# Expert slot numbers and gates fetched once ahead of the block loop; row gathers issued ahead of scatters; part of the last expert's first loads held back

## The reference, cut to what matters

```python
logits = (xf @ router_w + router_b)
top_vals, top_idx = lax.top_k(logits, TOP_K)          # 4 of 32 experts
gates = jax.nn.softmax(top_vals, axis=-1)
...
xb = xf[row_tok].reshape(n_blocks, MOE_BLOCK, D)      # rows of each expert, in blocks
h = xblk @ w1[e] + b1[e]                              # 1024 -> 2048
act = g * jax.nn.sigmoid(SWIGLU_ALPHA * g) * (u + 1.0)
y = act @ w2[e] + b2[e]                               # 1024 -> 1024
out = zeros.at[row_tok].add(y * row_w[:, None])
```

## Time and profile before

| | |
|---|---|
| median of 3 runs | 2829.48 us (2829.42 to 2830.85) |
| profiled execution | 2824.4 us |
| its span, first to last instruction | 2822.6 us |
| mean granted TensorE clock | 0.948 |
| PE busy | 2552.1 us (90%) |
| DVE, ACT, POOL busy | 744.7, 362.4, 499.3 us |
| bytes moved | 511.69 MB, mean 181 GB/s |
| routing ends, loop begins | about 985, 1009 us |
| last block's products end | about 2792 us |

### The profile page before, as it was taken

The page is one execution under the profiler, slowest core; times in us unless marked ns, Lnnn a source line. Parts: engine busy times, 40 slices in busy tenths (PEclk is TensorE's granted clock), DMA queues, the critical chain, the costliest instruction groups (busy, mean ns, idle before and its releaser), DMA issues.

```text
span 2822.6 us, 59253 instructions
## 1 busy us (share of the span) xinstructions
PE 2552.1 (90%) x22930; PEld 1090.6 (39%) x22931; DVE 744.7 (26%) x2075; ACT 362.4 (13%) x920; POOL 499.3 (18%) x639
## 2 busy tenths in 40 slices
PE   8999899999989769879998997997997999989984
PEld 4644556544435423223332332332332433323322
DVE  4441456411024412112221221221221222212212
ACT  2000455400003200000000000000000000000002
POOL 0000000000001212122221222221222222222221
PEclk9999899999999879889998998998998999999987
DMA  4110000400044495989689767668528357273464
GB/s 141 60 45 0 8 8 1 146 26 23 15 142 146 115 368 208 407 343 341 253 311 406 291 227 294 224 224 310 201 66 332 124 170 274 63 277 121 166 231 142
DMA packets 159463, 511.69 MB, mean 181 GB/s; under 512 B 37540, under 2 KB 73892, under 8 KB 125380
## 3 DMA queue, kind: packets, MB, share of 16 engines
q1 hardware_dynamic: 110576, 472.48, 43.1%
q0 software_dynamic: 29168, 38.39, 7.2%
q10 hardware_dynamic: 19668, 0.15, 0.4%
HBM read 479.16 MB, written 32.15 MB: 181 GB/s over the span
## 4 chain that ended last, share of the span: by engine, by line
PE 39%; DMA 23%; SPq 4%; issue 2%; DVE 1%; ACT 0%; ACTq 0%; POOL 0%; DVEq 0%; POOLq 0%
PE xbank L1487 21%; PE xbank L1510 13%; DMA big<-in_w 10%; DMA idxa<-slot_rows 9%; DMA loop_s<-xn_rows,idxg 4%; PE xbank L1443 4%; SPq L1034 2%; SPq L1039 1%; PE xbank L1497 1%; DMA acc_rows<-loop_s,idxs 0%; PE xbank L1504 0%; DVE big L1404 0%; PE xbank L1428 0%; DVE loop_s L1368 0%; ACT loop_s L1156 0%
## 5 line engine op out<-in xcount | busy, mean ns | idle before, releaser
L1487 PE MATMUL xbank<-big,loop_s 128*32 128x512 f32 x9280 | 1101.6, 612 | 134.0 <-DMA big<-in_w 109.9
L1487 PEld LDWEIGHTS xbank<-big,loop_s 128*32 128x32 f32 x9280 | 282.9, 111 | 788.2 <-issue 602.5
L1510 PE MATMUL xbank<-big,loop_s 128*32 128x256 f32 x9280 | 540.1, 386 | 0.0
L1368 DVE TENSOR_SCALAR loop_s<-xbank 128x256 f32<-128x256 f32 x145 | 61.6, 425 | 1301.3 <-PE xbank L1487 1301.3
L1510 PEld LDWEIGHTS xbank<-big,loop_s 128*32 128x32 f32 x9280 | 288.6, 112 | 247.7 <-issue 63.0
L1150 ACT ACTIVATE loop_s<-loop_s 128x256 f32<-128x256 f32 x145 | 60.5, 417 | 1658.7 <-DVE loop_s L1368 1635.4
L607 PE MATMUL pair<-big 128*128 128x512 f32 (+1 forms) x640 | 253.6, 551 | 0.2 <-DMA big<-in_w_in 0.2
L1086 POOL DMA_INDIRECT acc_rows<-loop_s,idxs x145 | 230.9, 1593 | 123.4 <-POOL idxs L1083 72.5
L1083 POOL TENSOR_TENSOR idxs<-idxa,tok 128x1 int32<-128x1 int32 x145 | 41.7, 288 | 941.9 <-ACT loop_s L1156 796.7
L1076 POOL DMA_INDIRECT loop_s<-xn_rows,idxg x147 | 145.8, 992 | 120.2 <-POOL idxg L1073 112.6
L607 PEld LDWEIGHTS pair<-big 128*128 128x128 f32 x640 | 119.3, 191 | 114.8 <-issue 110.8
(11 more groups left out here) (234 smaller groups left out, 1722.4 us busy)
## 6 DMA issues: line engine op xcount, KB each, us to landing
big<-in_w SPq DMA_DIRECT2D x396, 1024.0 KB, 12.9
big<-in_x SPq DMA_DIRECT2D x16, 512.0 KB, 5.0
big<-in_w_in SPq DMA_DIRECT2D x4, 2048.0 KB, 8.0
big<-in_w_in SPq DMA_DIRECT2D x16, 512.0 KB, 4.0
big<-in_w_o SPq DMA_DIRECT2D x1, 4096.0 KB, 26.9
acc_rows<-big SPq DMA_DIRECT2D x8, 512.0 KB
xn_rows<-big SPq DMA_DIRECT2D x8, 512.0 KB, 4.5
big<-acc_rows SPq DMA_DIRECT2D x8, 512.0 KB, 8.1
```

The lines of the kernel that those rows point to most:

```text
L1368: dve.tensor_scalar(gl, up_bank[b][:, 0:FG], SWIGLU_LIMIT, None, ALU.min).then_inc(gate_min, 1)
L1487: ins = pe.matmul(up_bank[b][QB * c:QB * c + QB, :].rearrange("p (h k q) -> p h k q", h=2, q=QB), xT[b][:, QB * k:QB * k + QB], w1k[b][k]. ...
L1510: ins = pe.matmul(y_bank[b][QB * j:QB * j + QB, 0:DG], actT[b][:, QB * k:QB * k + QB], w2r[b][:, k, j * DG:(j + 1) * DG], start=False, sto ...
```

## The change

1. The pair table is no longer read once for each block. When all scatters have landed and the block count is known, POOL issues two indirect DMAs that fetch all blocks' pairs, one partition for each block, 128 blocks a DMA (`raw`). VectorE takes them apart and adds the group numbers (`spread`), TensorE transposes four 128x128 tiles, and VectorE copies them to `idx_all` (row numbers of all blocks) and `gate_all`. `idx_ready` tells POOL and ACT. The table rows are worked out per partition (`row_i`) rather than in a list of one partition.
2. `load_slots` goes from ACT. `gather` takes a column of `idx_all` with a copy instead of an add.
3. POOL issues four gathers ahead of the loop, not three; in the loop gather(n+4) stands in front of scatter(n).
4. On DVE the wait for `y_done` and `choose` go in front of `swiglu` and `turn_x`.
5. On SP, W1 pieces 4 to 7 of the last expert wait for the first gather's rows (`xg_in[0]`), and W2 of the last expert comes behind them.

The diff, cut to its core:

```diff
             for k in range(4):
                 load_last(k)
 
+            sp.wait_ge(xg_in[0], 16)
+            for n in range(2):
+                sp.wait_ge(xn_out[n], 16 * NT // 2)
+            sp.wait_ge(list_ready, 1)
+            for k in range(4, KD):
+                load_last(k)
+
             sp.wait_ge(acc_out, 16 * NT)
             sp.wait_ge(rms2_ready, NT)
             sp.wait_ge(xn_ready, NT)
             for q in range(W2P):
                 sp.wait_ge(w2_in[q], 16)
                 sp.dma_start(w2q[1][q], w2_d[NEXP - 1, q]).then_inc(w2_in[q], 16)
-
-            sp.wait_ge(tab_out, 16 * NT * TOPK)
-            for n in range(2):
-                sp.wait_ge(xn_out[n], 16 * NT // 2)
-            sp.wait_ge(list_ready, 1)
-            for k in range(4, KD):
-                load_last(k)
 
             with sp.Fori(0, NEXP - 1) as j:
                 freed = sp.value_load(events[0:1, 0, bass.ds(j, 1)], min_val=1, max_val=NBLOCKS + 1)
...
                     pool.indirect_dma_start(out=tab_d, out_offset=bass.IndirectOffsetOnAxis(ap=posi[:, at:at + 1].bitcast(U32), axis=0),
                                             in_=pay[:, t, k, :], in_offset=None).then_inc(tab_out, 16)
 
-            def gather(n, b, half, reused):
-
-                pool.wait_ge(idx_in[b], half * 16 + 16)
+            def gather(n, b, reused):
+
                 if reused:
                     pool.wait_ge(xT_ready, n - 1)
-                pool.tensor_tensor(idxg[b][:, :], idxa[:, bass.ds(n, 1), 0], group, ALU.add).then_inc(idxg_ready, 1)
+                pool.tensor_copy(idxg[b][:, :], idx_all[:, bass.ds(n, 1)]).then_inc(idxg_ready, 1)
                 pool.wait_ge(idxg_ready, n + 1)
                 pool.sem_inc(gather_go, 1)
                 pool.indirect_dma_start(out=xg[b], out_offset=None, in_=xn_parts,
...
 
                 pool.wait_ge(y_taken, n + 3)
                 pool.wait_ge(rows_added, n * 16 + 32)
-                pool.tensor_tensor(idxs[b][:, :], idxa[:, bass.ds(n, 1), 0], group, ALU.add).then_inc(idxs_ready, 1)
+                pool.tensor_copy(idxs[b][:, :], idx_all[:, bass.ds(n, 1)]).then_inc(idxs_ready, 1)
                 pool.wait_ge(idxs_ready, n + 1)
                 pool.sem_inc(scatter_go, 1)
                 pool.indirect_dma_start(out=acc_parts, out_offset=bass.IndirectOffsetOnAxis(ap=idxs[b][:, :].bitcast(U32), axis=0),
                                         in_=yrow[b], in_offset=None, compute_op=ALU.add).then_inc(rows_added, 16)
-            pool.wait_ge(setup, 1)
             for n in range(2):
                 pool.dma_start(spare[:, 8 + n:9 + n], eps_c[0:1, :]).then_inc(rows_added, 16)
             pool.wait_ge(zero_out, 32)
             pool.wait_ge(acc_out, 16 * NT)
             for n in range(2):
                 pool.wait_ge(xn_out[n], 16 * NT // 2)
-            gather(0, 0, 0, False)
-            gather(1, 1, 0, False)
-            gather(2, 0, 1, True)
+            pool.wait_ge(tab_out, 16 * NT * TOPK)
+            pool.wait_ge(rows_ready, 1)
+            for c in range(2):
+                pool.indirect_dma_start(out=raw[:, c].rearrange("p q v -> p (q v)"), out_offset=None, in_=raw_d,
+                                        in_offset=bass.IndirectOffsetOnAxis(ap=row_i[:, c:c + 1].bitcast(U32), axis=0)).then_inc(raw_in, 16)
             n_iters = block_iters(pool)
+            pool.wait_ge(idx_ready, 1)
+            gather(0, 0, False)
+            gather(1, 1, False)
+            gather(2, 0, True)
+            gather(3, 1, True)
             with pool.Fori(0, PAIRS) as i:
                 with pool.If(i < n_iters):
-                    gather(i * 2 + 3, 1, i + 1, True)
+                    gather(i * 2 + 4, 0, True)
                     scatter(i * 2, 0)
-                    gather(i * 2 + 4, 0, i + 2, True)
+                    gather(i * 2 + 5, 1, True)
                     scatter(i * 2 + 1, 1)
             scatter(n_iters * 2, 0)
-            pool.wait_ge(xg_in[0], n_iters * 16 + 32)
-            pool.wait_ge(xg_in[1], n_iters * 16 + 16)
+            for n in range(2):
+                pool.wait_ge(xg_in[n], n_iters * 16 + 32)
 
         @block.scalar
         def _(act):
...
                 if 1 <= t <= NT:
                     store_xn(t - 1)
 
-            def load_slots(n, b, half):
-
-                if not (isinstance(half, int) and half == 0):
-                    act.wait_ge(idx_in[b], half * 16)
-                row = act.value_load(listi[0:1, 1, bass.ds(n, 1)], min_val=0, max_val=TABROWS - QB)
-                act.dma_start(idxa[:, bass.ds(n, 1), :].rearrange("p o v -> p (o v)"),
-                              tab_d[bass.ds(row, QB), :].unsqueeze(0).to_broadcast([NG, QB, 2])).then_inc(idx_in[b], 16)
-
             def sigmoid(n):
 
                 act.wait_ge(gate_min, n + 1)
...
 
                 act.wait_ge(y_done, n + 1)
                 act.wait_ge(rows_added, n * 16 + 16)
-                act.activation(yrow[b], y_bank[b][:, 0:DG], ACT.Copy, scale=gate_a[:, bass.ds(n, 1), 1]).then_inc(y_taken, 1)
+                act.activation(yrow[b], y_bank[b][:, 0:DG], ACT.Copy, scale=gate_all[:, bass.ds(n, 1)]).then_inc(y_taken, 1)
             act.sem_inc(y_taken, 2)
-            act.wait_ge(tab_out, 16 * NT * TOPK)
             n_iters = block_iters(act)
-            load_slots(0, 0, 0)
-            load_slots(1, 1, 0)
-            load_slots(2, 0, 1)
-            load_slots(3, 1, 1)
+            act.wait_ge(idx_ready, 1)
             sigmoid(0)
-            load_slots(4, 0, 2)
             with act.Fori(0, PAIRS) as i:
                 with act.If(i < n_iters):
                     for m in range(2):
-                        n = i * 2 + (m + 1)
-                        sigmoid(n)
+                        sigmoid(i * 2 + (m + 1))
                         weigh_y(i * 2 + m, m)
-                        load_slots(i * 2 + (m + 5), 1 - m, i + (2 + m))
             weigh_y(n_iters * 2, 0)
-            act.wait_ge(idx_in[0], n_iters * 16 + 48)
-            act.wait_ge(idx_in[1], n_iters * 16 + 32)
             for t in range(NT):
                 act.wait_ge(f_in[t], 16)
                 act.activation(fin_junk, fin[t], ACT.Square, accum_out=ss3[:, t:t + 1])
...
             dve.drain()
             dve.tensor_scalar(diag_t, ident[0:32, 0:32], t_c, None, ALU.mult).then_inc(time_ready, 1)
             dve.tensor_scalar(thr_c, t_c, 1.0, None, ALU.add)
-            dve.tensor_scalar(dummy_f, even_n[0:1, :], n_c[0:1, :], None, ALU.is_ge)
 
             dve.wait_ge(blocks_done, 1)
-            dve.scalar_tensor_tensor(out=row_f, in0=turn_q[0:1, :], scalar=float(QB), in1=bank[6][0:1, 0:NPAD], op0=ALU.mult, op1=ALU.add)
+            dve.tensor_tensor(row_2, turn_2, bank[6][:, 0:2], ALU.add)
+            dve.drain()
+            dve.scalar_tensor_tensor(out=row_i[:, :], in0=dummy_2, scalar=float(NEXP * S // QB), in1=row_2, op0=ALU.mult, op1=ALU.max)
+            dve.drain()
+            dve.sem_inc(rows_ready, 1)
             dve.tensor_copy(e_all[:, :], bank[2][0:96, 128:128 + NPAD])
-            dve.drain()
-            dve.scalar_tensor_tensor(out=listi[0:1, 1, :], in0=dummy_f, scalar=float(NEXP * S), in1=row_f, op0=ALU.mult, op1=ALU.max)
-            dve.drain()
-            dve.sem_inc(rows_ready, 1)
             dve.scalar_tensor_tensor(out=hot_p, in0=bank[6][0:32, 192:192 + NPAD], scalar=next_c, in1=not_odd_n,
                                      op0=ALU.subtract, op1=ALU.is_equal)
             dve.wait_ge(time_done, 1)
...
             dve.drain()
             dve.sem_inc(event_ready, 1)
             dve.wait_ge(event_done, 1)
-            dve.tensor_scalar(listi[0:1, 0, :], bank[7][0:1, 0:NPAD], 16.0, 16.0, ALU.mult, ALU.add)
+            dve.tensor_scalar(listi[0:1, :], bank[7][0:1, 0:NPAD], 16.0, 16.0, ALU.mult, ALU.add)
             dve.tensor_copy(events[0:1, :, :], bank[7][0:1, 192:288].rearrange("p (v j) -> p v j", v=3))
             dve.drain()
             dve.sem_inc(list_ready, 1)
-            dve.drain()
+
+            dve.wait_ge(raw_in, 32)
+            dve.tensor_copy(tok_n, raw[:, :, :, 0])
+            for c in range(2):
+                dve.tensor_copy(spread[:, 2 + c], raw[:, c, :, 1].bitcast(F32).unsqueeze(1).to_broadcast([P, NG, QB]))
+            dve.drain()
+            for c in range(2):
+                ins = dve.tensor_tensor(spread[:, c], tok_n[:, c].unsqueeze(1).to_broadcast([P, NG, QB]),
+                                        iota_e[:, 0:NG].unsqueeze(2).to_broadcast([P, NG, QB]), ALU.add)
+            ins.then_inc(spread_ready, 1)
+            dve.wait_ge(spread_turned, 1)
+            rest = 2 * P - NPAD
+            dve.tensor_copy(idx_all[:, 0:P], bank[4][:, 0:P])
+            dve.tensor_copy(idx_all[:, P:NPAD], bank[4][:, P + rest:2 * P])
+            dve.tensor_copy(gate_all[:, 0:P], bank[4][:, 2 * P:3 * P])
+            dve.tensor_copy(gate_all[:, P:NPAD], bank[4][:, 3 * P + rest:4 * P])
+            dve.drain()
```

(14 more changed lines are left out.)

63 lines of the change are left out of this document (37 added, 26 removed).

## The result

| | before | after |
|---|---|---|
| median | 2829.45 us (2827.67 to 2830.85, 4 runs) | 2762.89 us (2762.03 to 2771.35, 4 runs) |
| ratio | | 0.9772 (0.9752 to 0.9792) |
| profiled execution | 2824.4 us | 2771.35 us |
| its span | 2822.6 us | 2769.3 us |
| mean granted clock | 0.948 | 0.949 |

What follows compares the result with a forecast made beforehand. Bounds: late `sel` in lone switches, weight bytes in saturated stretches. From the profiled 2824.4 us, -38.4 + 2.0 - 3.0 + 8.3 = -31.1 gives 2793.3; plus 5.1 to the median, 2798.4 us, range 2785 to 2813.

Steps and rivals of the forecast that it cites:

- Nothing in a lone switch waits for weights: Loop, one slot changing expert at a time: TensorE's lost time there, 38.4 us, comes from `sel` waits and their clock.
- Part 1: Loop: slot loads out, gathers first, `choose` ahead of `turn_x`; `sel` waits go and lone switches lose their excess, -38.4 us.
- The +2 for late seventh pieces: Lone switches: W1's seventh piece late in four heavy switches at 0.5 us each, +2 us, bounds 0 and 7.
- rival A: Lone switches: weights take over as the limit and the gain there is lost, 2838 us or more; 6%.
- Part 2: Saturated stretches: the queue loses some 40 slot loads' packets at 0.076 us each, -3 us, bounds 0 and -12.
- Rival C: Saturated stretches: slot loads' packets sit on four engines only, so removal gives 12 us there, 2789 us total; 15%.
- The argument "against" C: Saturated stretches: the byte rate was already 406 GB/s, taken to speak against faster weight streams.
- A `sel` wait inside only moves idle time: Saturated stretches: bytes set the end, so no gain was counted from `sel` waits going there.
- Part 3: Start: last expert's held weight pieces leave the queue empty and delay all behind, +8.3 us, bounds +5 and +14.
- the sum with 14 us for the start: Start: pricing the 256 B fetches like 8-byte scatters at 10.0 us, start costs 14 us, sum 6 us more.
- B: Start: rows come at the slow end, the hold costs 14 us or more and late pieces 7, 2812 us; 12%.
- D: Loop: something else holds VectorE's queue, so half of the `sel` waits stay, 2819 us; 4%.

Runs made afterwards that it cites:

- experiment 4: Kernel after with VectorE's old order: 2766.15 us; with POOL's old order too: 2763.20 us. Kernel before with `choose` first: 2796.32 us.
- experiment 1: Kernel after plus one idle slot load a block on ScalarE, copied to four groups, read by nobody: 2856.78 us against 2764.11 us without.
- experiment 2: Kernel after plus one idle load a block, as 128 rows on 128 partitions: 2769.46 us; or as four 256 B packets: 2766.75 us.
- experiment 6: Kernel after, last expert's W2 first and unheld, W1 pieces 4 to 7 held only until fetched pairs are spread: 2759.69 us against 2764.11 us.

## Why the prediction was wrong in size

**The reading of what bounds the kernel** held: lone switches bound by `sel` and its clock, saturated ones by weights. "Nothing in a lone switch waits for weights" was true of the trace of before and hid that they were late there too; experiment 4 shows them as soon as `sel` is on time (136.1 us of waits for weights, and 12 us lost in lone switches).

**Part 1, -38.4 us**: -38.3. That it fits so well is in part luck: the orders, to which the prediction gave the gain, would have left 12 us of it (experiment 4). The +2 for late seventh pieces was not paid. The reason that the prediction gave for little slack, the landings of that switch, was itself a product of the slot loads. Windows over the same stretch of one lone switch, before and then after:

```profile
1313.00:1335.00 22.00, 20.85 (x268) 7.62 (x260) 4.67 (x12) 1.56 (x4) 5.43 (x9) 1.00 1.00 386
```
```profile
1313.00:1335.00 22.00, 22.00 (x284) 8.52 (x280) 5.23 (x14) 1.56 (x4) 6.98 (x10) 1.00 1.02 405
```

All DMAs together run at 405 instead of 386 GB/s (the weights alone at 381 instead of 368, and one gather more falls into the window), TensorE never stops, and rival A had no ground. The order, named as the cause of the `sel` waits, is half of it. They need rows that come late and `choose` behind them: they go when `choose` stands ahead (experiment 4, the kernel before) and also when the rows are early and `choose` stands last (experiment 4, the kernel after).

**Part 2, -3 us**: this is the step that failed. It was -20.4 in the profiled pair: -18.9 in the double switches up to the seventh piece, +2.3 behind it, -3.9 in the long stretch. The term was made from 0.4% of the engines' time, spread evenly over 16: 0.076 us a load. Four slot loads of the kernel before fall into each double switch up to the seventh piece, 24 in all, so it was 0.79 us a load there, ten times that. The idle loads of experiment 1 cost 1.6 us each at this place (38.0 us), half as many 1.5 (18.0 us), those of experiment 2, spread over 16 engines, 0.2 (4 us). Rival C had the right mechanism and, by its factor of four, 0.30 us a load, 12 us in all where the double switches up to the seventh piece and the long stretch gave 22.8. So the term had two things wrong: over how many engines the packets lie, and that their recorded time (some 9 ns each) is all that they take from the weights. What they take beyond it the records don't show. The argument "against" C was a misreading. A rate near 406 GB/s in a window doesn't speak against it: the same 8 us above have 407 GB/s in both kernels, though one is 0.8 us behind. A rate over all engines counts bytes, and TensorE waits for the slowest engine's part of one piece: 22.0, 23.2, 21.4 and 21.5 MB in the windows before, in experiment 1, after, and with spread loads.

**"A `sel` wait inside only moves idle time"** held: the doubles of the kernel before with `choose` first are no shorter (139 us against 134).

**Part 3, +8.3 us**: +5.0 in the profiled pair. The new path in after, from the chain in order of time; then the issues on SP (L1018 W1 of the last expert, L1034 its W2):

```profile
977.30 10.28 DMA slot_rows<-big
...
989.83 5.63 DMA loop_s<-slot_rows,row_i
...
996.57 1.13 PE xbank L1500 x4
...
998.52 0.19 POOL idxg L1081
...
999.49 2.79 DMA loop_s<-xn_rows,idxg
```
```profile
967.32 37.06 SPq L1018 DMA_DIRECT2D big<-in_w  x8
1004.54 2.13 SPq L1034 DMA_DIRECT2D big<-in_w  x4
```

Each step was faster than its estimate: the pairs landed at 995.5 (997 forecast), the row numbers were ready at about 998.5 (1001), the rows were there at 1002.3 (1006); the gather, for whose 3.9 us and lower bound of 3 the prediction had no row, took 2.79. So the fetches were no burden: the second took 5.63 us from its issue, and the sum with 14 us for the start is refuted. The Trainium skill, "DMA: Bandwidth & Descriptors", section "Specifications", has transfers below 512 B off line rate; for these few rows of 256 B nothing of it shows in the time. The held pieces were issued at 1002.3, and the first landed at 1007.5. The hole between weight landings, from 997.2 to 1007.5, is 10.3 us where 2.5 is usual, so 7.8 us; that was nearly right. But all pieces ahead of the hole were about 3 us earlier than before: the fourth landed at 997.2 and not at 1000.0. The 8.3 should have been 7.8 less 2.8. That nothing stands behind these pieces in the queue any more isn't the cause: with W2 behind them (experiment 6) the fourth landed 28.4 and 27.5 us after its issue, with nothing behind 26.8 to 28.2 us after it in four executions of the kernel after. The slot loads aren't the cause either: before with `choose` first has them at this place, and there it was 28.5 us. Only the profiled execution of before has 31.8. What made it so stays open.

**The execution.** The sum was put 5.1 us up to meet the median of before. The profiled execution of after lay 8.5 us above its own median, so the same step was wrong by 13.5 us, and 22 of the miss of 35.5 are due to the terms. In the first set the profiled execution of after took 2762.17, 9.2 less; by block ends 3.3 us of that lie in the start, 4.3 in the double switches and 1.4 behind the last block. The 4.3 are clock: behind the seventh pieces it is 36.8 against 42.1 us, up to them 204.0 against 202.9. What sets the clock there, and the start, stays open.

**Rivals.** A (2838), B (2812) and D (2819) didn't occur. C (2789) was nearest, 26 us too high.

**Open.** Experiment 1's loads cost 93 us, while splitting the loads of the kernel before gave 41. A part of this is that the split loads cost some 8 us themselves and that in the lone switches a part lay behind the `sel` waits, as experiment 4 shows. But up to the seventh pieces an idle load costs 1.6 us and a slot load of the kernel before 0.79. The idle loads are issued after each `weigh_y`, which comes at another time, and read other rows; neither was varied. Also open is what a small packet takes from its engine beyond its recorded time.

## What to carry to other kernels

Judge a small DMA beside a saturated stream by how many engines its packets lie on and how many packets each has to take, not by its bytes or its mean share: put a dimension of 16 or more outermost, or make it few large packets. Where a wait ends late in a trace, the ones behind it are not seen: before saying "nothing waits for weights", compare when the weights land with when they could be used, and expect to find a second cause of the same size. And before rewriting a step, try its smallest repair: splitting one DMA and moving two lines gave as much here as fetching the table in front of the loop with its hold (which by experiment 6 gains some 4 us more without most of that hold).
